# A moved row root, later memory splits and earlier weight halves in a two-layer encoder on one core

## The reference, cut to what matters

```
for i in (0, 1):
    if i == 1: k_shared, v_shared = heads of (rms_norm(h, kv_norm) @ w_kv)
    h = h + 0.5 * (silu(gate) * up) @ ffn1_w_down[i]      # gate, up = rms_norm(h) @ ffn1_w_gate_up[i]
    z = rms_norm(h, mix_norm[i]) @ w_in[i]                # 768 columns to mix, 256 for memory queries
    y_mix = pooling over windows 2, 4, 8, 16   (i = 0)
            or banded attention with sinks     (i = 1)
    y_mem = attention of 4 heads to rms_norm(mem, mem_norm[i]) @ w_mem_kv[i]
    h = h + concat(y_mix, y_mem) @ w_out[i]
    h = h + 0.5 * (silu(gate) * up) @ ffn2_w_down[i]      # the same form, with ffn2's weights
```

## Time and profile before

| | |
|---|---|
| median of 3 runs | 935.0 us (934.45 to 935.45) |
| profiled execution | 935.0 us, span 933.2 us |
| PE busy | 925.1 us (99% of the span) |
| DVE busy | 630.3 us (68%) |
| ACT busy | 499.4 us (54%) |
| POOL busy | 50.5 us (5%) |
| chain that ended last | PE 97%, DVE 1%, DMA 1% |
| DMA, mean over the span | 179 GB/s |

### The profile page before, as it was taken

The page is one execution under the profiler, slowest core; times in us unless marked ns, Lnnn a source line. Parts: engine busy times, 40 slices in busy tenths (PEclk is TensorE's granted clock), DMA queues, the critical chain, the costliest instruction groups (busy, mean ns, idle before and its releaser), DMA issues.

```text
span 933.2 us, 15026 instructions
## 1 busy us (share of the span) xinstructions
PE 925.1 (99%) x5041; PEld 786.1 (84%) x5041; DVE 630.3 (68%) x963; ACT 499.4 (54%) x746; POOL 50.5 (5%) x82
## 2 busy tenths in 40 slices
PE   8999999999999999999999999999999999999998
PEld 6788888888888888888888888888888888888887
DVE  5866566686567857566778866666877776675664
ACT  5744454464645545454464545446676555454542
POOL 2020120003000000000000000000221000000000
PEclk9999999999999999999999999999999999999999
DMA  8877556546136755656446765655433267555551
GB/s 272 273 220 230 192 178 203 181 146 215 46 99 216 220 187 184 198 168 216 136 153 208 219 196 170 221 183 181 144 127 114 72 218 228 182 183 191 170 176 45
DMA packets 136866, 167.02 MB, mean 179 GB/s; under 512 B 10776, under 2 KB 101632, under 8 KB 136832
## 3 DMA queue, kind: packets, MB, share of 16 engines
q1 hardware_dynamic: 135472, 164.67, 54.8%
q0 software_dynamic: 1184, 1.83, 0.8%
q10 hardware_dynamic: 176, 0.07, 0.0%
HBM read 165.48 MB, written 1.05 MB: 178 GB/s over the span
## 4 chain that ended last, share of the span: by engine, by line
PE 97%; DVE 1%; DMA 1%; SPq 0%; ACT 0%; issue 0%; ACTq 0%
PE ps L1568 30%; PE ps L1569 18%; PE ps L1706 8%; PE ps L1704 8%; PE ps L1702 8%; PE ps L1615 5%; PE ps L1617 5%; PE ps L1616 5%; PE ps L1571 4%; PE ps L1526 2%; PE ps L1834 1%; PE ps L1821 1%; DMA w_raw<-in_ffn_w_gate_up_dram 1%; PE ps L1865 1%; PE ps L1802 0%; PE ps L1854 0%
## 5 line engine op out<-in xcount | busy, mean ns | idle before, releaser
L1568 PE MATMUL ps<-mainT,w_hi 128*128 128x512 f32 (+1 forms) x1260 | 439.7, 393 | 2.4 <-DVE w_lo L1027 2.1
L1569 PE MATMUL ps<-mainT,w_lo 128*128 128x256 f32 (+1 forms) x1436 | 385.1, 278 | 0.0
L1027 DVE TENSOR_TENSOR w_lo<-w_raw,w_hi 128x1024 fp32r<-128x1024 f32 x296 | 350.1, 1220 | 45.0 <-ACT w_hi L662 44.4
L662 ACT CAST w_hi<-w_raw 128x1024 fp32r<-128x1024 f32 x296 | 298.9, 1047 | 25.4 <-PE ps L1571 11.5
L1568 PEld LDWEIGHTS ps<-mainT,w_hi 128*128 128x128 f32 x1260 | 236.3, 188 | 54.5 <-DVE w_lo L1027 3.2
L1569 PEld LDWEIGHTS ps<-mainT,w_lo 128*128 128x128 f32 x1436 | 271.1, 189 | 7.2
L715 ACT COPY gate_up_f<-ps 128x512 f32<-128x512 f32 x88 | 51.1, 581 | 113.1 <-PE ps L1571 107.6
L1111 DVE TENSOR_TENSOR gate_up_f<-ps,gate_up_f 128x256 f32<-128x256 f32 x88 | 37.3, 424 | 106.0 <-ACT gate_up_f L715 106.0
L1706 PE MATMUL ps<-w_hi,actT_lo 128*128 128x512 f32 x320 | 98.9, 390 | 0.0
L1704 PE MATMUL ps<-w_lo,actT_hi 128*128 128x512 f32 x320 | 98.9, 390 | 0.0
L1702 PE MATMUL ps<-w_hi,actT_hi 128*128 128x512 f32 x320 | 98.6, 389 | 0.0
(11 more groups left out here) (205 smaller groups left out, 820.6 us busy)
## 6 DMA issues: line engine op xcount, KB each, us to landing
w_raw<-in_ffn_w_gate_up_dram SPq DMA_DIRECT2D x352, 256.0 KB, 3.8
w_raw<-in_ffn_w_down_dram SPq DMA_DIRECT2D x176, 256.0 KB, 3.4
w_raw<-in_w_in_dram SPq DMA_DIRECT2D x32, 256.0 KB, 3.3
w_raw<-in_w_out_dram SPq DMA_DIRECT2D x32, 256.0 KB, 3.3
w_raw<-in_w_mem_kv_dram SPq DMA_DIRECT2D x16, 256.0 KB, 3.2
w_raw<-in_w_kv_dram SPq DMA_DIRECT2D x8, 256.0 KB, 3.7
ycat<-in_mem_dram SPq DMA_DIRECT2D x1, 1024.0 KB, 7.8
out_dram<-h SPq DMA_DIRECT2D x4, 256.0 KB, 2.0
```

What stands on the lines that cost most here:

```text
L662: ins = nc.scalar.copy(half(w_hi[s], b), half(w_raw[s], b))
L1027: ins = nc.vector.tensor_tensor(half(w_lo[s], b), half(w_raw[s], b), half(w_hi[s], b).bitcast(F32), ALU.subtract)
L1568: pe.matmul(dst[:, :, tokens], wh, both[:, k, :, tokens], start=start, stop=False)
L1569: mm = pe.matmul(dst[:, 0, tokens], wl, both[:, k, 0, tokens], start=False, stop=False)
```

## The change

It has five places.

- On POOL `row_roots("H0")` stands before the four DMAs of the second group of gain rows instead of behind them.
- In the second step of ffn0, the splits of mem for tile 1 stand behind the weight halves of gate unit 0, on ACT and DVE. TensorE turns tile 1 of mem inside `gate_up(1, 1)` at k = 4 instead of before it.
- At the end of ffn0, ffn1 and ffn2, ACT casts both halves of the next stage's first unit before `parts(f, last, 1)`; before, the second half came behind it. DVE does the first half before `gated(f, last, 1)` and the second before `act_low`; before, they came one place later each.
- In `split_out` on DVE the first low half of the next ffn stands before `probs_copy(7)`. For out0 the order stays the same.
- `first_piece` loses its tiles: k = 4 is one product over 256 tokens.

```diff
@@ -598,6 +598,7 @@
             nc.gpsimd.memset(head_gain_col[HD:HD + ROT, 2:3], 1.0).then_inc(ones_ready, 1)
             nc.gpsimd.memset(head_gain_col[HD:HD + ROT, 4:5], 1.0).then_inc(ones_ready, 1)
             pool.wait_ge(ones_ready, 5)
+            row_roots("H0")
             small = [
                 (inv_freq[:, :], a["c_inv_freq"].partition_broadcast(P)),
                 (pos_i[:, 0:1], a["positions"][0, 0:P].rearrange("(p o) -> p o", o=1)),
@@ -627,7 +628,6 @@
                 src = a[name].rearrange("l (k p) -> (l k) p", p=P) if n == 2 else a[name].rearrange("(k p) -> k p", p=P)
                 row = (first - FIRST_GAINS) * KC
                 pool.dma_start(gain_rows[1][row:row + n * KC, :], src).then_inc(gains_landed[1], 16)
-            row_roots("H0")
             assert len(small) == SMALL_LOADS
             for i, (dst, src) in enumerate(small):
                 pool.wait_ge(gu_done, 3 + i // 4)
@@ -782,10 +782,12 @@
                     parts(f, c, 0)
                     silu(f, c, 0)
                     if mem:
-                        for t in range(NT):
-                            for b in range(2):
-                                split("M", t, b)
+                        split("M", 0, 0)
+                        split("M", 0, 1)
                     high(name, gate[0], 0, turn=c + 1)
+                    if mem:
+                        split("M", 1, 0)
+                        split("M", 1, 1)
                     high(name, gate[1], 1, turn=c + 1)
                     parts(f, c, 1)
                     silu(f, c, 1)
@@ -806,10 +808,8 @@
                 silu(f, last, 0)
                 high(name, UNIT[name, "end"], None)
                 if FOLLOWING[name] is not None:
-                    high_unit(FOLLOWING[name], 0, (0,))
+                    high_unit(FOLLOWING[name], 0)
                 parts(f, last, 1)
-                if FOLLOWING[name] is not None:
-                    high_unit(FOLLOWING[name], 0, (1,))
                 silu(f, last, 1)
                 act.wait_ge(act_ready, (e0 + last) * 2 + 2)
                 nc.scalar.copy(endT_hi[:, :, :, :].rearrange("p c t n -> p (c t n)"),
@@ -1193,12 +1195,12 @@
                 gated(f, last, 0)
                 low(name, UNIT[name, "end"], None)
                 sums(f, last, 1)
+                if after is not None:
+                    low_unit(FOLLOWING[name], 0, (0,))
                 gated(f, last, 1)
                 if after is not None:
-                    low_unit(FOLLOWING[name], 0, (0,))
+                    low_unit(FOLLOWING[name], 0, (1,))
                 act_low(endT_lo, e0 + last)
-                if after is not None:
-                    low_unit(FOLLOWING[name], 0, (1,))
                 if after is None:
                     for t in range(NT):
                         residual(r, norm, t, 0)
@@ -1362,9 +1364,9 @@
 
             def split_out(name, l, after):
                 r = SUM_STAGES.index(f"out{l}")
+                low_unit(name, 0, (0,))
                 if l == 1:
                     probs_copy(7)
-                low_unit(name, 0, (0,))
                 residual(r, None, 0, 0)
                 if l == 1:
                     output(7)
@@ -1571,11 +1573,11 @@
                         mm = pe.matmul(dst[:, :, tokens], wh, both[:, k, :, tokens], start=False, stop=True)
                 return mm
 
-            def first_piece(k, fb, tile=None):
+            def first_piece(k, fb):
 
                 s, _ = UNIT["ffn0", k // 4]
                 if fb == 0:
-                    for t in range(NT) if tile is None else (tile,):
+                    for t in range(NT):
                         if k == 0:
                             pe.wait_ge(first_x_lo[t], 1)
                         elif k in (2, 4):
@@ -1584,7 +1586,7 @@
                         pe.wait_ge(lo_ready[s], k % 4 // 2 + 1)
                     else:
                         pe.wait_ge(first_lo, k // 2 + 1)
-                mm = gate_products(UNIT["ffn0", "gate"], k, fb, tile, k == 0, k == KC - 1)
+                mm = gate_products(UNIT["ffn0", "gate"], k, fb, None, k == 0, k == KC - 1)
                 if fb == 1 and k % 2 == 1:
                     mm.then_inc(weights_used[s], 1)
                 if fb == 0 and k == KC - 1:
@@ -1594,9 +1596,8 @@
                 turn_first(0, 1)
                 turn_first(1, 1)
                 for k in range(KC - 2):
-                    for tile in range(NT) if k == 4 else (None,):
-                        first_piece(k, 0, tile)
-                        first_piece(k, 1, tile)
+                    first_piece(k, 0)
+                    first_piece(k, 1)
                     if k == 1:
                         turn_h("H0", 0, 1)
                     elif k == 2:
@@ -1728,12 +1729,16 @@
                     turn_scales(f, norm)
                     gate_up(0, 1)
 
+                def memory_turns(k):
+                    if k == 4:
+                        turn_mem(1, 0)
+                        turn_mem(1, 1)
+
                 gate_up(1, 0)
                 if f == 0:
-                    for t in range(NT):
-                        for b in range(2):
-                            turn_mem(t, b)
-                gate_up(1, 1)
+                    turn_mem(0, 0)
+                    turn_mem(0, 1)
+                gate_up(1, 1, memory_turns if f == 0 else None)
                 if f == 0:
                     for t in range(NT):
                         for b in range(2):
```

## The result

The changed kernel takes 948.74 us (948.59 to 949.02, 4 runs) against 935.13 before; the ratio is 1.0147, 95% interval 1.013 to 1.0165. The change costs 13.6 us. The forecast was +9.9 (944.9) in a range to 947.8, which the time exceeds by 0.9: right in sign and place, too small in size. The profiled execution took 947.74 us for a span of 945.9, 12.7 us over the span before. The page of the profile: TensorE 928.2 us busy (98%), DVE 630.5, ACT 499.2.

The account below looks back on a forecast made before the run. TensorE, busy 925.1 of 933.2 us, was taken to bound the kernel, so new waits are paid in full. From 935.0, terms 5.4 + 0 + 1.1 + 2.9 + 0.5 = +9.9 gave 944.9 us; range 942.6 to 947.8.

Parts of the forecast that it names:

- Part A: Start, POOL: gain-row DMAs behind the roots of H0 delay TensorE's gain transpose from 19.46 to 24.84, +5.4 us.
- The clock: Rival: TensorE's clock falls in the stall at the gain transpose, slow products add 1.4 us, 946.3 us; chance 0.33.
- The chain behind A: Work queued behind the gain rows moves along; old weight waits at 25.23 and 27.70 return later and absorb nothing.
- Part B: ffn0's second step: two mem splits behind gate 0's weight halves delay the first down product, +1.1 us.
- Part C: Ends of ffn0, ffn1, ffn2: next weights ahead of last activations delay endT_lo and the end products, +2.9 us.
- Part D: Before the last values: ffn3's first low half ahead of the last probability copies makes TensorE wait, +0.5 us.
- Part E: First step, k = 4 in one piece: cost 0 under Part A's stall, 0.3 us without that cover.
- the dearest clock: Upper end of the clock rival: the clock stays low longer after the gain-transpose stall, up to 947.8 us.
- only A real: Rival: Part B, Part C and Part D stay inside their slack, only the gain-row stall counts, 940.4 us; chance 0.07.
- faster: Rival: early splits remove 2.1 us of weight waits, one-piece k = 4 saves 0.4, x lands sooner; 932.5 us; chance 0.015.

Follow-up runs that it names:

- Run eight: Kernel before with Part A, SyncE waiting for the gain rows before the second half of step 1's weight loads and mem's load: 938.2 us, ratio 1.0038.
- run seven: Kernel before with Part A, plus 26 unused products of zeros on TensorE before it waits for the gain rows: 941.75 us, ratio 1.0074.
- runs one: Kernel before with only the roots of H0 moved ahead of the four gain-row DMAs on GpSimd: 942.65 us, ratio 1.0084.
- ten: Kernel before with GpSimd issuing the gain-row DMAs only after the first half of x landed, still ahead of the roots: 934.62 us, ratio 0.9998.
- twelve: Kernel before with ffn0's first step reordered (weight casts earlier) and gain-row DMAs issued after the first half of x: 933.1 us, ratio 0.9983.

## Why the prediction was wrong

**Part A was the step that failed, by a term of its sum.** The stall, its place and its cause were as written. But the forecast took the landing of the last row as 3.7 us, its value at the start of the kernel; it was 5.6. In the terms of the step: last issue 20.34, not 20.99 (-0.65); landing 5.6, not 3.7 (+1.9); from landing to restart 0.1 instead of 0.15; resume at 26.04 instead of 24.84, so 6.58 us instead of 5.4. The bounds, 2.5 and 3.7, were both too low. The earlier issue is luck of the start: the second root ended at 18.72 in this execution and at 19.31 in that of before, and in the traces of all the runs between 18.68 and 19.44. With the forecast's issue time and the same landing A would have cost 7.2.

The prediction said "beside weight loads as it will here" and took the two situations as one. Before, SyncE had issued some 0.9 MB by 3.69 us (two weight loads of 256 KB, three pieces of x of 128 KB); in the changed kernel it had issued six weight loads and mem's 1 MB, 2.5 MB, in the 4.3 us before the last gain row. The share of busy DMA engines tells the two apart less well: 84% from 3.7 to 7.4 us in the kernel before, 94% from 20.34 to 26 in the changed one. Run eight shows that these loads are the cause: without them 1.7 us.

The Trainium skill (DMA: Bandwidth & Descriptors, Anatomy of one DMA) gives some 2.0 us for such a transfer, and run eight agrees with 1.7 to 2.0. In these traces that is the price on nearly idle DMA engines; with loads beside it the 4 KB row took 3.7 us or more in every one. The same page of the Trainium skill (Queues, rings and completion order) says that each DMA engine takes its queues in turn by packets, which fits a small transfer that waits without being shut out; no trace here shows the turns themselves.

**The clock is the second: it stood among the rivals, with 0.33, and not in the sum, and it came true.** It fell in each of the ten runs of the changed kernel and of A alone (mean clock 0.995 or 0.996). I had read the even chance out of the remark of the Trainium skill on the free-running gate (TensorE: Matmul & The Clock Gate, Part 1). For a stall of 6.8 us the ten runs don't bear that out; in run eight, with 3.1 us in its profile, two executions of five seem to have lost the full clock, as the remark would have it. The earlier trace rows had said 3 to 4 us of idleness, and the stall was 6.8; the row was the better guide. Its price was forecast as 1.4 and is 0.92 (run seven). The forecast took its slow product (0.45 us) from the kernel's start, for which the profile gives a granted clock of 1.00; that this was the low clock no row shows, but the 0.43 us at 0.50 in the changed kernel comes near it.

**The chain behind A** moved along as forecast, except that the low clock took 0.6 us of the first old wait.

**What a wait costs.** The idle time of a wait is counted from the end of the product before it, which the profile models. A 128x512 product lasts 0.39 us in these rows, but without a wait the next one starts 0.23 us after it; so a wait moves the next start by the idle time and another 0.16. Behind the wait the next start is 0.07 to 0.12 us late once more (the first product lasts 0.50), and the next ten products at the end of ffn1 lose another 0.06 in all. The steps of the table go from start to start, so each has this last loss of the wait before it.

**Part B**: forecast 1.1. Idle 1.12; TensorE's start moves by 1.28 across the wait (from 7.54 to 8.82 us late), and by 0.08 behind it. Mechanism and order of events as written.

**Part C**: forecast 1.42 + 0.75 + 0.75 = 2.9. The starts move by 1.36, 0.70 and 0.71 across the waits (idle 1.20, 0.54, 0.55), and by 0.14 to 0.18 behind each, where I had allowed 0.1; alone +3.5 by the median. The slack and the shifts were right to 0.1 us; the restart was too small.

**Part D**: forecast 0.5; the start moves by 0.46 across the wait (idle 0.30). +0.6 alone, not separable from nothing by the times. **Part E**: wait 0.9, shorter product, nothing net under A, as forecast; alone +0.4 beside 0.3, also not separable from nothing.

**The sum.** In the profiled execution, by the steps of the table: A 6.58, clock 0.92, B 1.32, C 3.19, D 0.64, in all 12.65 of 12.7. Against the forecast's 9.9 the differences are 1.2 (landing, less the earlier issue), 0.92 (clock), 0.2, 0.3 and 0.1. The median change is 13.6, another 0.9 above this execution. Part A alone spread over 941.5 to 943.4, more than the kernel before (0.7 to 1.3 us beside each set of runs), so the landing is a possible source, and so is the moment of the last issue, which hangs on the start. No profile of a slower execution was taken, and this remains open.

The range was too narrow on two counts. No bound of A held a landing above 3.7 us. And its upper end, 947.8, had the dearest clock (+2.9) on the middle of the sum; with the high ends of the parts (+1.1) added it would have been 948.9.

**The rivals that fell**: only A real (B and C measure 1.5 and 3.5 alone, and B to E together 5.7); faster (the gain rows landed at about 25.9, not by 19.46).

## What to carry to other kernels

In this kernel a small transfer on a waited-for path cost what the loads issued in front of it made it cost. Its landing time must be read where as many bytes were issued ahead of it as at the new place, or bounded from a contended row; here 1.7, 3.7 and 5.6 us were the same 4 KB. In an engine order written by hand each instruction moved forward has to be charged against the slack of what it passes (0.92 and 0.73 us here): look for the last slack, not for the first gain. Charge a new wait by starts, not by its idle time alone. Where a new stall passes the idle time after which the profile of before shows the clock falling, count the clock into the sum.

## What was not expected of the hardware

The same 4 KB transfer landed after 1.7 us (DMA engines 6% busy, run eight), 3.7 to 4.5 us (start of the kernel, 84 to 90% busy in the next 4 us) and 5.1 to 5.6 us (94% and more busy: the changed kernel and runs one, seven, ten and twelve).

A wait of TensorE cost more than its idle time: at the end of ffn1 0.54 us of idle made everything behind some 0.87 us later. 0.16 of it is that products no longer overlap across the wait, by the profile's modelled ends, 0.11 that the product behind the first one starts later (0.34 us after it instead of 0.23), and 0.06 that the next ones went out every 0.233 instead of 0.227 us.

The clock stayed full through an idle time of 3.1 us (profile of run eight; two other executions of it show a mean of 0.998) and fell in one of 6.8 us, between 3.7 and 4.7 us after the last product; back at work it was low for another 4.2 us.
